# Attention: a fourth probability buffer, one query tile moved to step 12, and value and query tiles ahead of the transposes of the probabilities

## The reference

```python
def chunk_attention(h, w_qkv, rel_bias, w_out):       # 16 heads of 64, chunks of 64 tokens
    q, k, v = split(h @ w_qkv)                        # q, k, v: (1, 1024, 16, 64)
    for c in range(nc):                               # each chunk of queries
        s = einsum('bqhd,bkhd->bhqk', q[c], k[c-8 .. c]) * scale + bias   # band of 9 chunks
        p = softmax(where(valid, s, -inf))
        o[c] = einsum('bhqk,bkhd->bqhd', p, v[c-8 .. c])
    return o @ w_out
```

## Time and profile before

| | |
|---|---|
| median of 3 runs | 2564.42 us (2560.94 to 2564.76) |
| the profiled execution's own time | 2565.88 us |
| its span, first to last instruction | 2563.9 us |
| mean granted clock of TensorE | 0.988 |
| PE busy | 96% of the span |
| DVE, ACT, POOL busy | 65%, 39%, 50% |
| attention, first scores to last values | 1291.9 to 1869 us |
| one of the six middle pairs | 74.1 us |

### The profile page before, as it was taken

One profiled execution on the slowest core, in us unless ns is written; L12 is line 12 of the kernel. 1 busy time (PEld: TensorE's weight loads), 2 busy tenths in 40 slices (PEclk: granted clock), 3 DMA queues, 4 the chain that ended last, 5 costly groups with the idle time before them and its releaser, 6 DMA issues. The chain is left out here.

```text
span 2563.9 us, 36363 instructions
## 1 busy us (share of the span) xinstructions
PE 2454.7 (96%) x11464; PEld 2026.0 (79%) x11464; DVE 1673.9 (65%) x2667; ACT 1011.0 (39%) x1831; POOL 1287.5 (50%) x898
## 2 busy tenths in 40 slices
PE   8998999999999999998989999999889999999987
PEld 7887888887788888886778787877777888888876
DVE  6246666667576777665866666676676677677755
ACT  5112211223434333331465555566644334433323
POOL 5242223223788787777312112221125878878776
PEclk9999999999999999999999999999989999999998
DMA  5232122101111211111110011111011111121111
GB/s 175 86 114 84 60 78 71 63 32 43 46 58 49 61 53 57 57 50 50 60 36 28 24 43 43 43 43 35 16 39 37 55 56 53 53 61 49 58 58 66
DMA packets 70522, 143.74 MB, mean 56 GB/s; under 512 B 7312, under 2 KB 17696, under 8 KB 69936
## 3 DMA queue, kind: packets, MB, share of 16 engines
q1 hardware_dynamic: 52912, 119.72, 14.5%
q10 hardware_dynamic: 17536, 23.07, 2.6%
HBM read 130.13 MB, written 12.63 MB: 56 GB/s over the span
## 5 line engine op out<-in xcount | busy, mean ns | idle before, releaser
L716 POOL TENSOR_TENSOR a_lo<-raw_block,a_hi 128x512 fp32r<-128x512 f32 x364 | 507.7, 1395 | 156.0 <-ACT a_hi L1604 131.6
L678 POOL TENSOR_SCALAR w_hi<-raw 128x1024 fp32r<-128x1024 f32 x80 | 90.6, 1133 | 823.3 <-PE bank L938 572.3
L1604 ACT ACTIVATE a_hi<-raw_block 128x512 fp32r<-128x512 f32 x324 | 202.4, 629 | 332.0 <-PE bank L938 121.5
L936 PE MATMUL bank<-T_hi,a_hi 128*128 128x512 f32 x672 | 262.5, 391 | 3.8 <-issue 3.3
L938 PE MATMUL bank<-T_hi,a_lo 128*128 128x512 f32 x672 | 261.6, 389 | 0.0
L937 PE MATMUL bank<-T_lo,a_hi 128*128 128x512 f32 x672 | 261.5, 389 | 0.0
L936 PE MATMUL bank<-B_hi,a_hi 128*128 128x512 f32 x576 | 224.9, 390 | 2.7 <-DVE h_full L2071 1.7
L938 PE MATMUL bank<-B_hi,a_lo 128*128 128x512 f32 x576 | 224.2, 389 | 0.0
L937 PE MATMUL bank<-B_lo,a_hi 128*128 128x512 f32 x576 | 224.1, 389 | 0.0
L680 POOL TENSOR_TENSOR w_lo<-raw,w_hi 128x1024 fp32r<-128x1024 f32 x80 | 199.5, 2493 | 6.7
L2071 DVE TENSOR_TENSOR h_full<-bank,h_full 128x512 f32<-128x512 f32 x54 | 37.3, 691 | 211.6 <-PE bank L938 198.1
(11 more groups left out here) (282 smaller groups left out, 6585.5 us busy)
## 6 DMA issues: line engine op xcount, KB each, us to landing
raw_block<-f_blocks_in SPq DMA_DIRECT2D x176, 256.0 KB, 2.6
raw<-w_units_in SPq DMA_DIRECT2D x80, 512.0 KB, 3.4
raw_block<-f_down_in SPq DMA_DIRECT2D x72, 256.0 KB, 3.0
v_raw<-v_scratch ACTq DMA_DIRECT2D x16, 512.0 KB, 3.9
bias<-rel_scratch ACTq DMA_DIRECT2D x8, 640.0 KB, 3.7
x<-x_t_in SPq DMA_DIRECT2D x16, 256.0 KB, 5.6
v_scratch<-atmp ACTq DMA_DIRECT2D x16, 256.0 KB, 2.4
v_scratch<-full ACTq DMA_DIRECT2D x16, 256.0 KB, 2.7
```

What stands on the lines that cost most here:

```text
L678: pool.tensor_scalar(w_hi[slot][:, :], raw[r][:, :], 1.0, 1.0, ALU.mult, ALU.mult).then_inc(w_split, 1)
L716: pool.tensor_tensor(out, full, r32(hi), ALU.subtract).then_inc(made, 1)
L936: pe.matmul(out, lh, rh, start=start, stop=False, skip_group_check=read_between)
L1604: act.activation(a_hi[pos][:, :], src[:, :], ACT.Copy).then_inc(w.left_hi, 1)
```

## The change

The change does four things.

- There are four probability buffers in all pairs but the last, which keeps three (`probs(last)`). The fourth, `prob3`, lies in the memory of `tmp`, which the last pair needs for its squares. With four, the bias addition of step m waits for the transposes of s = m - 4, issued one step before, and no longer for those of s = m - 3.
- `NEXT_Q` has one of its three tiles of step 13 in step 12.
- In each step PE issues the tiles of the values, the transposes of the values and the tiles of the queries ahead of `transpose_probs`.
- ACT does the `o_move` of step 12 ahead of `pt_hi` and the scaling of that step, in place of behind them.

```diff
-        prob = [sb(f"prob{i}", d_at + 2560 * i, [P, WIN]) for i in range(3)]
+
+        prob = [sb(f"prob{i}", d_at + 2560 * i, [P, WIN]) for i in range(3)] + [sb("prob3", s_at, [P, WIN])]
...
-        NEXT_Q = [{4: (0,), 6: (1,), 8: (2,), 10: (3,), 13: (4, 5, 6), 14: (7,)}, {16: (0, 1), 17: (2,), 18: (3, 4), 19: (5,)}]
+        NEXT_Q = [{4: (0,), 6: (1,), 8: (2,), 10: (3,), 12: (4,), 13: (5, 6), 14: (7,)}, {16: (0, 1), 17: (2,), 18: (3, 4), 19: (5,)}]
...
+        def probs(last):
+            return 3 if last else 4
...
-            def transpose_probs(it, s):
+            def transpose_probs(it, s, last):
...
-                    t = pe.transpose(probs_t[:, j * P:(j + 1) * P], prob[s % 3][:, j * P:(j + 1) * P], ident[:, :])
+                    t = pe.transpose(probs_t[:, j * P:(j + 1) * P], prob[s % probs(last)][:, j * P:(j + 1) * P], ident[:, :])
...
                     if m < 16:
                         scores_of(it, m)
-                    if 0 <= m - LAG < 16:
-                        transpose_probs(it, m - LAG)
                     for k in V_1.get(m, ()):
                         part(it, "v", 1, k, u + 2, 2)
...
                         for k in NEXT_Q[h].get(m, ()):
                             part(it, "q", h, k, u + 3, 3)
+                    if 0 <= m - LAG < 16:
+                        transpose_probs(it, m - LAG, last)
                     for n in OUT1P.get(m, ()) if not first else ():
                         out_product(it, "out1p", n, 0)
...
                                        accum_out=rowsum[:, c]).then_inc(exp_done, 1)
+                    if m == 12:
+                        o_move(1)
                     if 0 <= m - LAG < 16:
...
-                    if m in (8, 12, 16, 19):
+                    if m in (8, 16, 19):
                         o_move((m - 7) // 4)
...
-                        ge(dve, t_done, it * 16 + (m - 2))
+                        ge(dve, t_done, it * 16 + (m - probs(last) + 1))
```

More of the change, by code:

```diff
@@ L186, in trunk @@
         rv = small("rv", [P, BLOCKS])
[L187 to L190, removed]
+        rowmax = small("rowmax", [P, 4])
+        negmax = small("negmax", [P, 4])
+        rowsum = small("rowsum", [P, 4])
+        rowinv = small("rowinv", [P, 4])
         std_col = small("std_col", [P, HALF // P])
@@ L1840, in attention @@
                         off = window(s)
-                        c = slice(s % 3, s % 3 + 1)
+                        b = s % probs(last)
+                        c = slice(b, b + 1)
                         act.wait_ge(neg_done, it * 16 + (s + 1))
-                        act.activation(prob[s % 3][:, off:], prob[s % 3][:, off:], ACT.Exp, bias=negmax[:, c],
+                        act.activation(prob[b][:, off:], prob[b][:, off:], ACT.Exp, bias=negmax[:, c],
                                        accum_out=rowsum[:, c]).then_inc(exp_done, 1)
+                    if m == 12:
+                        o_move(1)
                     if 0 <= m - LAG < 16:
@@ L1852, in attention @@
                         s = m - 2
-                        c = slice(s % 3, s % 3 + 1)
+                        b = s % probs(last)
+                        c = slice(b, b + 1)
                         act.wait_ge(inv_done, it * 16 + (s + 1))
-                        act.activation(prob[s % 3][:, window(s):], prob[s % 3][:, window(s):], ACT.Copy,
+                        act.activation(prob[b][:, window(s):], prob[b][:, window(s):], ACT.Copy,
                                        scale=rowinv[:, c]).then_inc(normed, 1)
@@ L2469, in attention @@
                         s = m - 2
-                        c = slice(s % 3, s % 3 + 1)
+                        c = slice(s % probs(last), s % probs(last) + 1)
                         dve.wait_ge(exp_done, it * 16 + (s + 1))
@@ L2474, in attention @@
                         off = window(m)
-                        c = slice(m % 3, m % 3 + 1)
+                        b = m % probs(last)
+                        c = slice(b, b + 1)
                         dve.wait_ge(qk_done, it * 16 + (m + 1))
@@ L2478, in attention @@
                             dve.wait_ge(bias_masked, it * 2 + 2)
-                        ge(dve, t_done, it * 16 + (m - 2))
+                        ge(dve, t_done, it * 16 + (m - probs(last) + 1))
                         dve.sem_inc(step_begun)
-                        dve.tensor_tensor_reduce(prob[m % 3][:, off:], scores[:, SHIFT + off:SHIFT + WIN],
+                        dve.tensor_tensor_reduce(prob[b][:, off:], scores[:, SHIFT + off:SHIFT + WIN],
                                                  bias[:, step(m)[1], off:], 1.0, -3.0e38, ALU.add, ALU.max,
```

## The result

The changed kernel takes 2610.76 us (median of 4 runs, 2604.28 to 2615.15) against 2564.59 us of the kernel before, run beside it: a ratio of 1.0182 (95% interval 1.0168 to 1.0195). It is 46 us slower. The forecast was 2606 us. The profiled execution took 2609.44 us, 1.9 us more than the 2607.5 us that the sum gave for it.

A forecast was written before the change was run, and what follows sets the result against it. PE, busy 96% of the span, bounds the kernel. Stalls of 31.6 us (4.6 in six middle pairs, 4.0 in the first) plus clock 10 took 2565.88 to 2607.5 profiled, forecast 2606 us; 8-in-10 range 2576 to 2624.

The forecast's parts named there:

- (a): Steps 3 and 4: low part of the values comes later, first query tile waits for it; loss 0.9 us a middle pair.
- (b): Steps 6 to 11: transposes 0.69 us later in even steps, PE then waits for `pt_lo`; loss 0.5 us a middle pair.
- steps 12 and 13: Query tile moved into step 12's stall saves 0.5 us, step 13 loses 0.1 us waiting for `o_lo`: -0.4 us together.
- (c): Steps 14 to 19: late transposes delay the queries' low part, `pt_lo`, `o_full` and `values`; loss 3.6 us a middle pair.
- clock: New stalls drop PE to half clock: 1.4 us a pair, one stretch in most, 10 us for seven pairs.
- Fourth buffer: Bias addition freed from the latest transposes: removes most of PE's stalls of 0.36 and 1.06 us in steps 11 and 13.
- rival A: Delaying the transposes is free, only removed stalls count: faster by about 11 us, 2554 us; chance 0.12.
- Tile in step 12: A tile's 0.69 us moves from step 13 into step 12's stall; step 13's first product then waits 1.1 us for `o_lo`.
- B: Only step 16 bites, the rest is caught up, no clock fall: 2582 us; 0.17 including what lies up to the forecast.
- C: Clock falls twice or more in each pair, steps 3 to 4 and 16 to 17: 2631 us; chance 0.10 with beyond.
- D: DVE's own order holds the bias addition back, buffer gains nothing: 2616 us, or no change; chance 0.03 inside the range.

The follow-up runs named there:

- all transposes first: Changed kernel with transpose_probs back ahead of the tiles in every step; four buffers, query tile in step 12 and early o_move stay: 2554.23 us, 0.9963.
- the last two edits: Against all transposes first: tiles ahead of the transposes in step 13 only, 2555.62 us; DVE's o_add of step 12 ahead of pt_lo, 2555.55 us; both, 2545.78 us.
- step 16 was filled: Changed kernel plus eight matmuls with unread results in step 16 of every pair but the last, ahead of its query tile: 2610.51 us, 1.0179.
- step 17 was filled: Changed kernel plus four matmuls with unread results in step 17 of every pair but the last, ahead of its transposes: 2601.47 us, 1.0146.
- in its three forms: Changed kernel with transposes ahead of the tiles: nothing else changed, 2554.23 us; three buffers, 2563.98 us; four buffers, query tile back in step 13, 2556.17 us.
- the three of the last section: All transposes first plus tiles ahead in step 13 only, 2555.62 us; plus o_add of step 12 ahead of pt_lo, 2555.55 us; plus both, 2545.78 us.

## Why the prediction was right, step by step

The mechanism held. The total came out close, 41.6 us predicted and 43.4 measured for the profiled execution, but in part by luck: two terms were off with opposite signs. Measured is how much later each step starts in a middle pair, by the first scores, than in the kernel before, in pairs without a fall of the clock:

| part of a middle pair | predicted | measured |
|---|---|---|
| (a) steps 3 and 4 | +0.9 us | +1.04 us |
| (b) steps 5 to 11 | +0.5 us | +0.68 us |
| steps 12 and 13 | -0.4 us | -0.17 us |
| (c) steps 14 to 19 | +3.6 us | +3.9 us |
| sum | 4.6 us | 5.46 us |
| clock, six middle pairs | 8.4 us (1.4 each) | 5.8 us |

- **Fourth buffer.** Right: the wait for the transposes fell from 20.8 us to one of 1.0 us, in the last pair. Its worth, 9 us under the old order, is near what rival A had put, in part by chance: a middle pair gained 0.9 us with all transposes first, where A had 1.5.
- **Tile in step 12.** The mechanism was right: the first product of step 13 waits 1.16 us for `o_lo`, predicted 1.1. Steps 12 and 13 together were mis-sized a little, -0.17 us in place of -0.4.
- **(a)** Timeline of the kernel after, fourth pair, steps 3 and 4:

```profile
1542.38 0.66 PE L1398 MATMUL bank<-ident,atmp 128*128 128x128 f32 x4 [0.92 <-DVE atmp L2434]
...
1545.29 0.49 PE L940 MATMUL bank<-B_hi,w_hi 128*128 128x512 f32 x1 [0.99 <-DVE v L2410]
```

The first query tile waits 0.99 us for the low part of the values, as forecast.
- **(c)** Right in its order and its sizes. Step 16 waits 1.97 us for the low part of the queries (2.1 predicted), step 17 1.05 us for `pt_lo` (1.2), and `values` 0.74 us for `o_full`. Before, these waits were 0.59 us for the queries, and the transposes stood ahead.
- **The clock.** The weak step. Its size was too large (8.4 us for the six middle pairs; 5.8 us measured). Four of the six fall, so the pairs are not evenly longer, as I expected, but by 5.5 to 7.1 us. The prediction took the falls to belong to all the stalls of steps 16 and 17, and a little to those of steps 3 and 4; in the middle pairs nothing falls at steps 3 and 4. It also took its 3.5 us from part of a longer fall: in the last pair of the kernel before the granted clock is 0.50 from 1860.6 to 1867.4, 6.8 us. Each fall of the middle pairs lasted 3.4 us, so the half that it used fitted, and that was luck. The stalls' sum, 5.46 us in place of 4.6, was 6 x 0.86 = 5.2 us too small; the clock in the same pairs was 2.6 us too large. The first pair took 5.3 us more, where 4.0 and 1.4 were predicted.
- **Rival A** fell at the place that it named: PE reaches step 16's tile with the queries not ready. Its 2554 us is the time of the kernel in which nothing is delayed (2554.23). **B**, 2582 us, is close to the kernel with tiles ahead in step 16 alone (2577.85), which says what B left out: the steps before 16 cost as much again. Nor is what follows step 16 caught up, as B had it: in that kernel PE waits 1.75 us more in step 17. **C** did not come, **D** neither.

The rule of the Trainium skill ("TensorE: Matmul & The Clock Gate", Part 3, "The mechanism") that matmuls start in program order is borne out. In step 16 the transposes of s = 13 could have run once `pt_lo` had freed `probs_t`, at 1579.52 + 0.82 = 1580.34 (ACT had scaled their input by 1580.20), while PE stood idle until 1581.82 at a tile ahead of them; and the order in that step alone was worth 23 us.

## What to carry to other kernels

On an engine that works in order, put what starts another engine's chain (here the transposes) ahead of work that only fills, and a filler ahead only where it is ready and the other is not. Before a piece is moved into a stall, look for what PE will then reach too early: the tile in step 12, and each of the last two edits alone, mostly moved a wait. The two edits paid when each took away the wait that the other had made.

## What the runs showed of the hardware

- Of six pairs with the same stalls, some kept full clock and some did not: behind idle of 1.05 and 0.74 us with five transposes between, three of six fell to half clock (and three of six where step 16 was filled), and behind idle of 1.97 us one of six (two of six where step 17 was filled). In the profiles of the eight kernels without the late transposes of step 16 (before; all transposes first, in its three forms; ahead from step 16 on; the three of the last section) no middle pair fell, 48 in all. The longest single wait in their middle pairs was 0.6 to 1.24 us, by kernel. A stretch of 3.4 us at half clock cost 1.6 us in step 17 and 1.05 us in step 16, where PE would else have waited longer for `pt_lo`.
- Filling a stall with matmuls that no one reads shortened the program (9 us, step 17) in one place and did nothing in another (step 16). What decides in which pair the clock falls is open.
